# MoE results added to gathered residual rows and stored by indirect DMA, in place of scatter products on TensorE

## Reference, cut to what matters

```
x = x + mixed @ w_out
x = x + hier_moe(rmsnorm(x, norm_moe_g), ...)
y = rmsnorm(x, norm_final_g)

def hier_moe(x):                      # 320 tokens
    p_top, grp = top_1(softmax(x @ w_rg + b_rg))           # one of 4 router groups per token
    top_vals, top_idx = top_2(logits of the 8 experts in that group)
    combine = softmax(top_vals) * p_top, spread over 32 experts
    y = 0
    for e in range(32):
        hidden = silu(x @ w_g[e]) * (x @ w_u[e])           # 1024 -> 256
        y = y + combine[:, e] * (hidden @ w_d[e])          # 256 -> 1024
    return y
```

## Time and profile before

| | us |
|---|---|
| runs | 885.08, 887.18, 887.42; median 887.18 |
| span of the profiled execution | 885.9 |
| PE busy, share of the span | 861.3, 97% |
| DVE busy | 604.2, 68% |
| ACT busy | 473.2, 53% |
| POOL busy | 59.1, 7% |
| DMA moved | 186.35 MB, mean 210 GB/s |
| DVE L1763 and L1771, 128 x 512, mean | 0.68 |
| ACT L1299, square of 128 x 512, and its accumulator read | 0.63 and 0.19 |
| POOL's last product (L1973) ends at | 878.08 |
| slot weights: the chain before them ends on DVE, PE starts them | 578.05, 581.20 |
| ACT's first DMA issues end, its first copy that PE needs starts | 3.93, 7.32 |
| issue to landing of the stores of y (L570), medians | 3.8 and 4.5 |

### The profile page before, as it was taken

One profiled execution on the slowest core, in us unless ns is written; L12 is line 12 of the kernel. 1 busy time (PEld: TensorE's weight loads), 2 busy tenths in 40 slices (PEclk: granted clock), 3 DMA queues, 4 the chain that ended last, 5 costly groups with the idle time before them and its releaser, 6 DMA issues. The chain is left out here.

```text
span 885.9 us, 13071 instructions
## 1 busy us (share of the span) xinstructions
PE 861.3 (97%) x5213; PEld 779.3 (88%) x5213; DVE 604.2 (68%) x828; ACT 473.2 (53%) x621; POOL 59.1 (7%) x126
## 2 busy tenths in 40 slices
PE   6999999999999999999999999999999999999994
PEld 5998989999989989999999998988888887887882
DVE  5665487773544456695565556578898989899875
ACT  4664377753333324454333344356777677767663
POOL 3302011120011011000000000100000000000002
PEclk9999999999999999999999998789999999999998
DMA  9756433334334345345446471679999999999941
GB/s 269 213 183 240 137 126 108 108 119 146 97 130 156 118 137 190 102 144 161 136 143 238 143 240 46 232 247 356 341 362 352 347 350 353 350 356 355 351 171 62
DMA packets 100003, 186.35 MB, mean 210 GB/s; under 512 B 5288, under 2 KB 71104, under 8 KB 99936
## 3 DMA queue, kind: packets, MB, share of 16 engines
q1 hardware_dynamic: 95648, 172.78, 57.3%
q0 software_dynamic: 3488, 10.48, 3.6%
q10 hardware_dynamic: 800, 2.18, 0.6%
HBM read 178.28 MB, written 7.14 MB: 209 GB/s over the span
## 5 line engine op out<-in xcount | busy, mean ns | idle before, releaser
L1389 DVE TENSOR_TENSOR unit_r<-arena,unit_r 128x2048 fp32r<-128x2048 f32 x63 | 144.9, 2299 | 140.1 <-ACT unit_r L1006 139.9
L1398 DVE TENSOR_TENSOR w_r<-arena,w_r 128x2048 fp32r<-128x2048 f32 x96 | 216.8, 2286 | 32.4 <-ACT w_r L1017 32.4
L580 PE MATMUL pj<-xn_r,unit_r 128*128 128x320 f32 x1536 | 235.0, 311 | 0.0
L580 PEld LDWEIGHTS pj<-xn_r,unit_r 128*128 128x128 f32 x1536 | 225.5, 188 | 5.7 <-issue 3.6
L890 PE MATMUL pj<-w_r,xg 128*128 128x512 f32 x768 | 192.4, 401 | 0.0
L1017 ACT ACTIVATE w_r<-arena 128x2048 fp32r<-128x2048 f32 x96 | 180.1, 1909 | 0.0
L890 PEld LDWEIGHTS pj<-w_r,xg 128*128 128x128 f32 x768 | 142.7, 190 | 30.6 <-ACT xg L1243 0.2
L1006 ACT ACTIVATE unit_r<-arena 128x2048 fp32r<-128x2048 f32 x63 | 120.1, 1907 | 23.9 <-PE pj L580 20.0
L919 PE MATMUL pj<-w_r,hidT 128*128 128x512 f32 x384 | 93.3, 392 | 1.1 <-ACT hidT L1256 0.6
L919 PEld LDWEIGHTS pj<-w_r,hidT 128*128 128x128 f32 x384 | 71.9, 188 | 17.7 <-DVE w_r L1398 1.4
L580 PE MATMUL pj<-br_r,unit_r 128*128 128x320 f32 x384 | 59.6, 311 | 0.0
(11 more groups left out here) (364 smaller groups left out, 833.4 us busy)
## 6 DMA issues: line engine op xcount, KB each, us to landing
arena<-in_w_in SPq DMA_DIRECT2D x40, 1024.0 KB, 5.2
arena<-in_w_exp_gate SPq DMA_DIRECT2D x64, 512.0 KB, 4.4
arena<-in_w_exp_up SPq DMA_DIRECT2D x64, 512.0 KB, 5.7
arena<-in_w_exp_down SPq DMA_DIRECT2D x64, 512.0 KB, 4.9
arena<-in_w_mem_v SPq DMA_DIRECT2D x4, 1024.0 KB, 6.3
arena<-in_w_br_mem SPq DMA_DIRECT2D x4, 1024.0 KB, 5.1
arena<-in_w_br_mlstm SPq DMA_DIRECT2D x4, 1024.0 KB, 5.2
arena<-in_w_br_gmlp SPq DMA_DIRECT2D x4, 1024.0 KB, 5.2
```

The source lines that it names most:

```text
L580: last = mm(bank_of(s)[0:out_rows, 0:out_cols], l, r, start=k == 0, stop=k == len(pairs) - 1)
L1389: v.tensor_tensor(unit_r[n % RING][:, 1, :], ringw[:, n % RING, :], unit_r[n % RING][:, 0, :], ALU.subtract).then_inc(u_lo, 1)
L1398: v.tensor_tensor(w_r[u % NS][:, 1, :], raw_w[u % NS], w_r[u % NS][:, 0, :], ALU.subtract).then_inc(m_lo, 1)
```

## The change

x_rows now holds x itself, and the MoE gain is applied in three other places: to hnT on its way out of PSUM, and to the slot rows xg. Each group's sums are added to the gathered rows in slot order, the final norm is done per group on the slot rows, and POOL stores the rows to y_rows (320 x 1024) by indirect DMA. The row number of a slot comes from a second column of the token product, biased by 512 so that an empty slot falls out of bounds. yo, ohT, the scatter products, the one-hot transposes, gm_g and y_tm are gone. The host splits y_rows in two views.

```diff
@@ gather, transpose, split of slot rows @@
+            act.dma_start(gpk[:, :], I["norm_moe_g"][0, :].rearrange("(p k) -> p k", k=KC)).then_inc(s_gpk, 16)
-                        act.dma_start(gm_g, I["norm_moe_g"][0, :].partition_broadcast(128)).then_inc(s_gm, 16)
-                            sp.wait_ge(s_xs, 3 + 9 + j + 1)
-                            sp.dma_start(x_rows[t0:t0 + n, :], xs_tm[0:n, i, :]).then_inc(s_rows, 16)
+                            sp.wait_ge(*done("res", 3, i))
+                            sp.dma_start(x_rows[t0:t0 + n, :], x_tm[0:n, i, :]).then_inc(s_rows, 16)
@@ residual adds on DVE @@
-                    if (u, i) == (0, 0):
-                        dve.wait_ge(s_gm, 16)
-                    dve.wait_ge(*done("res", u, i))
-                    cs = slice(u * 256, u * 256 + 256)
-                    v.tensor_tensor(xs_tm[0:n, i, cs], x_tm[0:n, i, cs], gm_g[0:n, cs], ALU.mult).then_inc(s_xs, 1)
-                    v.tensor_copy(hnT[:, c, :], b[:, 0:T]).then_inc(free, 1)
+                    v.tensor_scalar(hnT[:, c, :], b[:, 0:T], prT[:, P_MOE + c:P_MOE + c + 1], None, ALU.mult).then_inc(free, 1)
@@ ACT, slot rows @@
-                    af(xg[g % 2][:, 4 * half:4 * half + 4, 0, :], banks[:, 2 + half, :]..., ACT.Copy).then_inc(m_xgh, 1)
+                    for j in range(4):
+                        k = 4 * half + j
+                        af(xg[g % 2][:, k, 0, :], banks[:, 2 + half, j * SLOTS:(j + 1) * SLOTS], ACT.Copy, scale=gpk[:, k:k + 1]).then_inc(m_xgh, 1)
@@ DVE, slot rows @@
+            def output_rows():
+                v.tensor_scalar(slot_out[:, 0:1], ms[:, 3, 1:2], float(NO_ROW), None, ALU.add).then_inc(m_outrow, 1)
+                v.tensor_scalar(slot_out[:, 1:G], pj[:, 0, 0:2 * G]..., float(NO_ROW), None, ALU.add).then_inc(m_outrow, 1)
...
-                    v.tensor_tensor(x_[:, :, 1, :], banks[:, 2 + half, :]..., x_[:, :, 0, :], ALU.subtract).then_inc(m_xgl, 1)
+                    for j in range(4):
+                        k = 4 * half + j
+                        ins = v.scalar_tensor_tensor(xg[g % 2][:, k, 1, :], banks[:, 2 + half, j * SLOTS:(j + 1) * SLOTS], gpk[:, k:k + 1], xg[g % 2][:, k, 0, :],
+                                                     ALU.mult, ALU.subtract)
+                    ins.then_inc(m_xgl, 1)
@@ PE, level @@
-                    if 1 <= x <= G:
-                        onehots_T(lv, x - 1)
                     if x in ROWS_AT:
                         slot_rows_T(lv, ROWS_AT[x])
-                    if g and e >= 2:
-                        scatter(lv, g - 1, e - 2)
                 hidden_T(lv, E - 1)
                 down(lv, E - 1)
-                for o in range(6):
-                    scatter(lv, G - 1, o)
@@ ACT, level @@
-                    if g and e == 1:
-                        y_high(lv, g - 1)
                     if x + 1 < E:
                         unit_high(lv, AT[x + 1, "A"])
-                    if 2 <= x <= G + 1:
-                        onehots_T(lv, x - 2)
+                    if g and e == 2:
+                        group_squares(lv, g - 1)
+                    elif g and e == 4:
+                        group_deviation(lv, g - 1)
...
-                y_high(lv, G - 1)
-                for k, o in enumerate(OUTS_OF[G - 1][0:5]):
-                    ...
+                group_squares(lv, G - 1)
+                group_deviation(lv, G - 1)
+                act.wait_ge(m_grs, 5 * (G * lv + G))
+                act.wait_ge(m_ygain, 2 * lv + 1)
+                y_ = xrow[:, (G - 1) % 3, 0:512]
+                af(y_, y_, ACT.Copy, scale=rs[:, G - 1:G]).then_inc(m_yfin, 1)
@@ ACT, new @@
+            def group_squares(lv, g):
+                for half in range(2):
+                    act.wait_ge(m_yadd, 2 * (G * lv + g) + half + 1)
+                    af(squares[:, g % 3, half * 512:half * 512 + 512], xrow[:, g % 3, half * 512:half * 512 + 512], ACT.Square, scale=D ** -0.5, accum_out=...).then_inc(m_gss, 1)
+            def group_deviation(lv, g):
+                act.wait_ge(m_gvar, G * lv + g + 1)
+                af(sd[:, g:g + 1], var[:, g:g + 1], ACT.Sqrt).then_inc(m_gsd, 1)
@@ DVE, new; group_variance is one op, group_scale reciprocal and four small ops, each waiting for the one before @@
+            def y_add(lv, g, half):
+                ...
+                x_ = xrow[:, g % 3, half * 512:half * 512 + 512]
+                v.tensor_tensor(x_, x_, pj[:, 2 + half, :], ALU.add).then_inc(m_yadd, 1)
@@ DVE, level @@
                     if g and e == 1:
-                        y_rest(lv, g - 1)
+                        y_add(lv, g - 1, 0)
+                        y_add(lv, g - 1, 1)
+                    elif g and e == 3:
+                        group_variance(lv, g - 1)
+                    elif g and e == 5:
+                        group_scale(lv, g - 1)
+                        y_ = xrow[:, (g - 1) % 3, :]
+                        v.scalar_tensor_tensor(y_, y_, rs[:, g - 1:g], nf_g[:, :], ALU.mult, ALU.mult).then_inc(m_yfin, 1)
...
-                    if g and g < G and e >= 3:
-                        add_result(lv, g - 1, e - 3)
-                    elif g >= 2 and e == 0:
-                        add_result(lv, g - 2, 5)
...
+                y_add(lv, G - 1, 0)
+                y_add(lv, G - 1, 1)
+                y_ = xrow[:, (G - 1) % 3, :]
+                for half in range(2):
+                    dve.wait_ge(m_gss, 2 * (G * lv + G - 1) + half + 1)
+                    v.tensor_tensor(y_[:, cs], y_[:, cs], nf_g[:, cs], ALU.mult).then_inc(m_ygain, 1)
+                group_variance(lv, G - 1)
+                group_scale(lv, G - 1)
+                dve.wait_ge(m_ygain, 2 * lv + 2)
+                v.tensor_scalar(y_[:, 512:D], y_[:, 512:D], rs[:, G - 1:G], None, ALU.mult).then_inc(m_yfin, 1)
@@ POOL; gather_rows(lv, 3) now waits for m_yout[0], the first group's store @@
+            def rows_out(lv, k):
+                pool.wait_ge(m_yfin, (G + 1) * lv + k + (2 if k == G - 1 else 1))
+                pool.indirect_dma_start(O["y_rows"], bass.IndirectOffsetOnAxis(slot_out[:, k:k + 1], 0), xrow[:, k % 3, :], None,
+                                        bounds_check=T - 1, oob_is_err=False).then_inc(m_yout[k], 16)
+            def level(lv):
+                for k in range(3):
+                    gather_rows(lv, k)
+                pool.wait_ge(m_outrow, 2 * lv + 2)
+                rows_out(lv, 0)
+                gather_rows(lv, 3)
+                for k in range(1, G):
+                    rows_out(lv, k)
+                for k in range(G):
+                    pool.wait_ge(m_yout[k], 16 * lv + 16)
```

More of the change, by code:

```diff
@@ L411, in build_kernel @@
         slot_token = sb("slot_token", [128, G], U32)
+        slot_out = sb("slot_out", [128, G], U32)
+        gpk = sb("gpk", [128, KC])
         x_rows = nc.dram_tensor("x_rows", (T, D), FP32, kind="Internal").ap()
@@ L563, in _ @@
                             load_unit(lv, u)
[L564 to L571, removed]
         @block.tensor
@@ L802, in _ @@
                     c, = a
-                    for j, i in enumerate(RES_ORDER[c // 2]):
+                    for i in RES_ORDER[c // 2]:
                         t0, n = TILES[i]
-                        pe.wait_ge(s_xs, 3 + 3 * (c // 2) + j + 1)
-                        last = tr(b[:, t0:t0 + n], xs_tm[0:n, i, c * 128:(c + 1) * 128], ident[0:n, 0:n])
+                        pe.wait_ge(*done("res", c // 2, i))
+                        last = tr(b[:, t0:t0 + n], x_tm[0:n, i, c * 128:(c + 1) * 128], ident[0:n, 0:n])
                 elif kind == "ranks":
@@ L822, in slot_tokens @@
             def slot_tokens(lv):
[L824 removed]
+                until(pe, m_xgl, 2 * G * lv)
                 if isinstance(lv, int):
@@ L837, in slot_rows_T @@
                 if g == 0:
[L838 to L842, removed]
+                    until(pe, m_yadd, 2 * G * lv)
+                else:
+                    pe.wait_ge(m_xgl, 2 * (G * lv + g))
+                if g == 1:
+                    for e in "AD":
+                        pe.wait_ge(freed["hx", e], _seen["hx", e])
                 pe.wait_ge(m_row[g], 16 * lv + 16)
@@ L861, in slot_weights @@
                 last.then_inc(m_comb, 1)
[L863 to L869, removed]
             def gate_up(lv, x, part):
@@ L887, in gate_up @@
                 for j, (k, xp, wp) in enumerate(order):
+                    if x % EPG == 0 and j < 8 and wp == 0:
+                        pe.wait_ge(m_xgh, KC * (G * lv + g) + k0 + k + 1)
                     if x % EPG == 0 and j == 8:
@@ L923, in down @@
                 last.then_inc(m_used, 1)
[L925 to L942, removed]
             def level(lv):
@@ L1221, in _ @@
                     c, = a
-                    af(hnT[:, c, :], b[:, 0:T], ACT.Copy).then_inc(free, 1)
+                    af(hnT[:, c, :], b[:, 0:T], ACT.Copy, scale=prT[:, P_MOE + c:P_MOE + c + 1]).then_inc(free, 1)
                 elif kind == "moe_var":
```

(26 more changed lines are left out.)

137 lines of the change are left out of this document (44 added, 93 removed).

## The result

The changed kernel took 878.85 us (median of four runs, 877.16 to 878.96) beside 887.3 us for the kernel before; the ratio is 0.9905 with a 95% interval of 0.9884 to 0.9926, so 8.5 us less. The forecast was 876.9 in a range of 872.5 to 884.0. A second set of four runs gave 877.11 (875.15 to 879.38). The profiled execution has a span of 876.9 against 885.9.

The account below looks back on a forecast made before the run. PE was taken to bound the expert stretch, dependent steps the tail. Routing -0.6, first expert +0.2, stretch -6.9 and tail -3.0 sum to -10.3 us: span 875.6 from 885.9, plus 1.3 gives 876.9 us, range 872.5 to 884.0.

Parts of the forecast that it names:

- Routing, -0.6: Before the experts: 0.4 us from the gain multiply and 0.2 from the other multiplies leaving DVE, 0.6 us less in sum.
- the gain multiply leaves the path: Between the last residual add and the last hnT transposes: DVE's 0.42 us multiply goes, 0.4 us less.
- First expert, +0.2: Gain on slot rows means smaller ACT and DVE pieces; later work moves by about 1 us, D0 by 0.2 us.
- Stretch, PE: Experts: 18 scatters out, -8.3 us; one-hot transposes out, -1.2; sixth residual add at starts of groups 2 and 3 out, -1.1.
- DVE's block, +2.7: At e = 5, five small DVE steps and a product ahead of hidden_rest make D 0.9 us late, three times.
- Tables, 0: At e = 4 a square root between silus adds two 1.28 us ACT table loads per group, absorbed by waits: 0.
- the rival that made ACT stand still longer: Around e = 4 and 5: a second 1.28 us standstill at each table load, DVE and ACT become the pace; 880.1 us, chance 0.10.
- Weight stream, +1.0: Expert stretch: DMA ceiling at 350 to 365 GB/s is near, so a backlog costs 1.0 us, ends 0 and +5.
- The rival in which the stream is the bound already: Expert stretch: with a ceiling of 350 GB/s it gives -1.1 us for -6.9, time 882.7 us; chance 0.15.
- signs of being wrong: ACT waiting for DMA, granted clock leaving 1.00, indirect store landing over 7 us after issue, or expert period above 8.8 us.
- Tail, -3.0: After the last down product: the end comes 3.0 us earlier, at 882.8, with 1.9 us taken for POOL's DRAIN.
- the slower side: Expert stretch: new PE waits drop its clock to 1.2 GHz, 3.3 us each; six falls cost 20 us, 896.7 us; chance 0.05.

Follow-up runs that it names:

- t2: Changed kernel with SP, not POOL, waiting for the four last stores, and POOL reading the level count ahead of the last store; 875.00 us.
- p1: Changed kernel with two unread 512-column matmuls put where each of the 18 removed scatter products stood; 885.95 us.
- s1: Changed kernel with the square root in the scale of groups 0 to 2 replaced by a copy, so their scale is wrong; 878.01 us.
- b2: Changed kernel with DVE's five small steps moved behind the rest of hidden at e = 5 and the product to the same place at e = 6; 877.95 us.
- t1: Changed kernel with SP, not POOL, waiting for the four last stores; 874.66 us.
- d2: Changed kernel with 512 KB more stored per group in the stretch, to a tensor nobody reads; 879.45 us.

## Why the prediction was right, and where it wasn't

Of its 10.3 us of span 9.0 came, but the sum came that close partly by luck, as misses of both signs met in it. The front gave nothing where 0.4 was forecast, and the end 1.4 for 3.0; the stretch gave 7.6 for 6.9 and so covered a part of that. By its steps:

- **Routing, -0.6.** It did not come. PE takes its work in order, and two rows that the working left out decide it. The kernel before, then after:

```profile
560.14 1.56 PE L609 MATMUL ms<-wr,arena 128*128 128x36 f32 x12
560.34 0.42 DVE L1652 TENSOR_TENSOR arena<-arena,pj 128x256 f32<-128x256 f32 x1 [2.56 <-PE pj L668]
```

```profile
559.63 1.56 PE L599 MATMUL ms<-wr,arena 128*128 128x36 f32 x12
559.83 0.42 DVE L1619 TENSOR_TENSOR arena<-arena,pj 128x256 f32<-128x256 f32 x1 [2.50 <-PE pj L658]
```

  PE's router matmuls run until 561.70 and 561.19, and the transposes start at 561.64 and 561.12, in both 1.3 us behind the last add. The multiply lay beside them, so the step "the gain multiply leaves the path" failed. In the profiles with the clock pattern of before (0.69 from 534 to 545) the way from w_out's first product to ACT's first xg copy is 60.0 to 60.2 us (60.07 in t2, 60.12 in p1) against 59.96.
- **First expert, +0.2.** It held: from that copy to D0 16.37 us became 16.59. Conversions and comb moved by 1.1 us as the step said (comb's copy from 586.28 to 587.36).
- **Stretch, PE.** Held: 8.46 to 8.61 us in the plain experts of groups 1 to 3, and p1 confirms the price. D1 to D4 took 1.2 us less together, D16, D17, D24 and D25 1.1 less, as forecast.
- **DVE's block, +2.7.** Held: D12, D20 and D28 are 0.84 late, 2.5 together, and 2.8 with what follows. That "one expert later" DVE has absorbed it is nearly so; 0.1 is left each time.
- **Tables, 0.** Held (s1), and the rival that made ACT stand still longer fell.
- **Weight stream, +1.0.** Mis-sized: 0. The ceiling was read off a rate that was demand. With the other terms as they came the stretch to the end of the last down product fell by 7.6 us for the 6.9 forecast. The rival in which the stream is the bound already has fallen for this kernel. Its mechanism appears only when the stalls are taken out (b2, D17). Two of the forecast's signs of being wrong did come: ACT waited for weights (1.1 us), and three of the four stores landed 9.0 us after their issue, beyond the 7 named. Neither moved the end: D16 and D17 are on time, and the one store in the tail landed in 3.4.
- **Tail, -3.0.** It gave -1.4, and that is the term that failed: "Ends 0.1 and 3.9; no row is nearer, so I take 1.9". DRAIN took 4.16, above the upper end. The 3.85 of the earlier trace rows were POOL's own, and no row could say so. From the last product's end to the scaled rows the sum gave 4.4 and 4.3 came; issue and landing gave 4.25 for 4.7, the count load and branches 1.8 for 1.6, the barrier 0.2 for 0.35.
- **Clock.** The granted clock stayed at 1.00 through the stretch; waits of 0.6 to 0.75 us did not lower it, so the slower side did not come up.

The profiled execution's time is 2.0 us above its span, 1.3 was taken; that 0.7 and the span's 1.3 (876.9 for 875.6) are the 1.95 us between the forecast and the measured time.

## What to carry to other kernels

Where one engine is busy without a gap, count what leaves it in full, and then look for what the others, now with less cover, have in one block: here 2.8 us came back through one badly placed block on DVE. Two halves fit where the whole did not, and a stall removed can take away the time in which a transfer caught up. Look at the way out as well: the engine that waits for the last transfer should be one whose exit is short, and POOL's isn't. A transfer rate is a ceiling only once more has been asked of it.

## What the runs showed of the hardware that was not expected

POOL's DRAIN at the exit takes some 3.9 to 4.6 us of its own (SP's took 0.01 us in t1), whether or not a transfer is under way. In d2 the DMA engines moved 392 GB/s for 30 us, with weights, stores and a gather together. An indirect row store that landed in 3.4 us on quiet queues (the last one) took 9.0 beside the weight stream (the three before it). And one wait of PE near 536 us was followed by three different clock patterns (0.69, 0.84 and 1.00 of the full clock over 11 us) in kernels that are the same up to there, two of them in two profiles of the very same kernel; with what else varies in the front, that shifts D0 by up to 3.6 us. Why they differ stays open.
